# A post-norm decoder layer: smaller selection allowance ahead of normalisations, first carried sum ahead of the rotation, weights in two loads, values last in TensorE's band steps

## The reference

```
proj = x @ w_in + b_in
dq, dk, dv, iq, ik, iw, sq, sk, sv = split(proj)          # rope on dq, dk, iq, ik, sq, sk
score[t, s] = sum_h iw[t, h] * relu(iq[t, h] . ik[s])     # s <= t, 8 index heads
keep the 256 best keys of each query; softmax attention over them, 8 heads share dk, dv
sliding-window attention of 128 keys over sq, sk, sv, 8 heads, 2 key heads, sinks
x = LN(a*x + concat(both) @ w_o)
x = LN(a*x + cross_attention(x, mem))                     # 4 heads of 256, 256 memory tokens
x = LN(a*x + square(relu(x @ w_up)) @ w_down)
```

## Time and profile before

| | us |
|---|---|
| median of 3 runs | 1494.96 |
| lowest and highest | 1489.4, 1495.07 |
| the profiled execution, its own time | 1495.45 |
| its span, first to last instruction | 1493.6 |
| mean granted TensorE clock | 0.993 |

### The profile page before, as it was taken

The page is one execution under the profiler, slowest core; times in us unless marked ns, Lnnn a source line. Parts: engine busy times, 40 slices in busy tenths (PEclk is TensorE's granted clock), DMA queues, the critical chain, the costliest instruction groups (busy, mean ns, idle before and its releaser), DMA issues.

```text
span 1493.6 us, 21073 instructions
## 1 busy us (share of the span) xinstructions
PE 1451.2 (97%) x7552; PEld 1238.0 (83%) x7552; DVE 1070.8 (72%) x2091; ACT 499.6 (33%) x1050; POOL 750.3 (50%) x583
## 2 busy tenths in 40 slices
PE   7999998999899999999999999999999999999997
PEld 7878788999899987888878788888888888888885
DVE  6678899888886334944339677776777777777757
ACT  3135688988776521212202212111111111111111
POOL 4340368677500033044430676766677767867612
PEclk9999999999899999999999999999999999999999
DMA  6446266666310053021111012020201111020202
GB/s 245 165 146 169 85 210 197 177 193 204 108 43 1 1 191 99 22 85 57 57 48 37 7 51 85 3 84 29 85 29 57 57 57 57 29 85 1 85 29 85
DMA packets 61478, 128.98 MB, mean 86 GB/s; under 512 B 6976, under 2 KB 34112, under 8 KB 53696
## 3 DMA queue, kind: packets, MB, share of 16 engines
q1 hardware_dynamic: 51008, 108.76, 22.2%
q10 hardware_dynamic: 10368, 18.88, 3.5%
HBM read 100.35 MB, written 27.26 MB: 85 GB/s over the span
## 4 chain that ended last, share of the span: by engine, by line
PE 91%; DVE 5%; POOL 2%; issue 1%; ACT 1%; DMA 0%; DVEq 0%; ACTq 0%; SPq 0%; POOLq 0%
PE banks L903 25%; PE banks L905 25%; PE banks L904 25%; PE banks L1112 4%; PE banks L960 3%; PE banks L961 2%; PE banks L1099 2%; PE banks L1121 2%; PE banks L1068 2%; POOL w_lo L814 1%; PE banks L1048 1%; POOL w_hi L809 1%; DVE score L1817 0%; DMA raw<-w_v_dram 0%; DVE h_buf L2197 0%
## 5 line engine op out<-in xcount | busy, mean ns | idle before, releaser
L809 POOL TENSOR_SCALAR w_hi<-raw 128x512 fp32r<-128x512 f32 x156 | 103.7, 693 | 409.5 <-PE banks L905 211.1
L2322 DVE TENSOR_TENSOR h_buf<-h_buf,banks 128x512 f32<-128x512 f32 x320 | 202.5, 678 | 13.2 <-PE banks L905 9.7
L814 POOL TENSOR_TENSOR w_lo<-raw,w_hi 128x512 fp32r<-128x512 f32 x156 | 206.9, 1359 | 0.0
L903 PE MATMUL banks<-act_hi,w_hi 128*128 128x512 f32 x512 | 199.9, 390 | 1.7 <-DVE act_lo L2176 1.7
L904 PE MATMUL banks<-act_lo,w_hi 128*128 128x512 f32 x512 | 199.9, 390 | 0.0
L905 PE MATMUL banks<-act_hi,w_lo 128*128 128x512 f32 x512 | 199.8, 390 | 0.0
L903 PE MATMUL banks<-seven_hi,hid_hi 128*128 128x512 f32 x392 | 152.6, 389 | 0.0
L904 PE MATMUL banks<-seven_lo,hid_hi 128*128 128x512 f32 x392 | 152.5, 389 | 0.0
L905 PE MATMUL banks<-seven_hi,hid_lo 128*128 128x512 f32 x392 | 152.5, 389 | 0.0
L903 PE MATMUL banks<-w_hi,act_hi 128*128 128x512 f32 x384 | 152.1, 396 | 0.0
L905 PE MATMUL banks<-w_hi,act_lo 128*128 128x512 f32 x384 | 149.8, 390 | 0.0
(11 more groups left out here) (222 smaller groups left out, 3489.0 us busy)
## 6 DMA issues: line engine op xcount, KB each, us to landing
raw<-w_down_dram SPq DMA_DIRECT2D x16, 1024.0 KB, 4.7
raw_up<-w_up_dram SPq DMA_DIRECT2D x14, 1024.0 KB, 4.8
q_tile<-qk_dram SPq DMA_DIRECT2D x176, 64.0 KB, 2.7
qk_dram<-q_hi ACTq DMA_DIRECT2D x28, 256.0 KB, 2.1
qk_dram<-roped ACTq DMA_DIRECT2D x28, 256.0 KB, 2.6
x_raw<-x_t_dram SPq DMA_DIRECT2D x8, 512.0 KB, 8.9
raw<-wk_mem_dram SPq DMA_DIRECT2D x4, 1024.0 KB, 5.1
raw<-wv_mem_dram SPq DMA_DIRECT2D x4, 1024.0 KB, 5.8
```

The costliest lines, as they stand in the source:

```text
L809: pool.tensor_scalar(w_hi[s][:, col], source[:, col], 1.0, 1.0, ALU.mult, ALU.mult)\
L814: pool.tensor_tensor(w_lo[s][:, col], source[:, col], w_hi[s][:, col].bitcast(F32), ALU.subtract).then_inc(w_ready, 1)
L903: pe.matmul(dst, lh, rh, start=(first and n == 0), stop=False)
L2322: ins = dve.tensor_tensor(out, out, ring_m[g % 6][:], ALU.add if way > 0 else ALU.subtract)
```

## The change

The budget of the band steps gets four values by n % 4 instead of one. SP loads the first weights in two pieces, the first quarter (400 of 1600 columns) first, with a semaphore of its own, for which ACT waits ahead of the first piece; it waits for the rest ahead of the second. In the odd halves DVE does the first carried sum ahead of rope_second. PE's band step does the transposes ahead of the first memory product, and any third product ahead of the values.

```diff
-NARROW_EARLY, BUDGET_BAND = 0.9, 2.1
+NARROW_EARLY = 0.9
+BUDGET_BAND = [2.5, 2.5, 2.5, 0.9]
...
-            sp.dma_start(raw[0][:, 0:columns_of(0)], source_of(0)).then_inc(raw_in[0], 16)
+            rest = slice(v_piece(1).start, columns_of(0))
+            sp.dma_start(raw[0][:, v_piece(0)], source_of(0)[:, v_piece(0)]).then_inc(v_first_in, 16)
+            sp.dma_start(raw[0][:, rest], source_of(0)[:, rest]).then_inc(raw_in[0], 16)
...
                 pieces = pieces_at(n)
+                if 0 <= n - 3 < NS:
+                    swa_turn(n - 3)
                 for use, piece in pieces[0:1]:
                     memory_product(use, piece)
-                if 0 <= n - 3 < NS:
-                    swa_turn(n - 3)
                 if 0 <= n - 2 - NS < ND:
                     turn_probs(n - 2 - NS)
                 for use, piece in pieces[1:2]:
+                    memory_product(use, piece)
+                for use, piece in pieces[2:]:
                     memory_product(use, piece)
                 if 0 <= n - 4 < NS:
                     swa_values(n - 4)
                 if 0 <= n - 3 - NS:
                     times_values(n - 3 - NS)
-                for use, piece in pieces[2:]:
-                    memory_product(use, piece)
...
             round_x(0)
+            act.wait_ge(v_first_in, 16)
+            round_v_weights(0)
             act.wait_ge(raw_in[0], 16)
-            round_v_weights(0)
...
                 carried = index_carried(v + 1)
+                for n in carried[0:1]:
+                    index_sum(n)
                 rope_second(r)
                 for part in range(2):
-                    for n in carried[part:part + 1]:
+                    for n in carried[1:2] if part else ():
                         index_sum(n)
                     if r < POOL_SPLIT:
                         split_roped(r, part)
...
-                    select_for(BUDGET_BAND if n < NS else BUDGET_DSA[DSA[min(n - NS, ND - 1)][0]], True)
+                    select_for(BUDGET_BAND[n % PAIRS] if n < NS else BUDGET_DSA[DSA[min(n - NS, ND - 1)][0]], True)
```

More of the change, by code:

```diff
@@ L508, in build_layer @@
         mem_in = sem("mem_in")
+        v_first_in = sem("v_first_in")
         x_in = sems("x_in", NK)
```

## The result

The changed kernel takes **1509.31 us** (median of six runs, 1502.69 to 1510.53); the kernel before, beside it, 1492.12 us (1488.68 to 1495.07). The ratio is 1.0105, 95% interval 1.0086 to 1.0124: slower by about 1%. The same kernel beside the later experiments took 1506.92 us against 1493.04, ratio 1.0090 (1.0073 to 1.0106). The forecast was 1505, with 1495 to 1511 around it.

A forecast was written before the change was run, and what follows sets the result against it. PE was taken to bound the kernel, busy 1451.2 of 1493.6 us. Terms -0.2 + 7.0 + 3.4 - 1.0 - 0.3 + 1.4 = +10.3 on the median of 1494.96 gave 1505 us, range 1495 to 1511.

The forecast's parts named there:

- The forecast's case: Whole kernel: new PE waits in the index stage, low clock behind, a late split in step 35; 1505 us, chance 0.57.
- Early sum: Index stage, halves 10 to 16: rotation waits for the first rectified score, delaying PE; +6.75, with DVE's queueing +7.0 us.
- small queueing of DVE: Index stage: small extra on DVE that takes the sum of the halves from +6.75 to +7.0 us.
- Half 16: Index stage: score already rectified, so PE's 2.71 us wait moves one score on; gain 0.2 us, bounds 0 and 1.
- Its clock: PE's clock in the index stage: two of three new waits followed by 1.7 us lost; +3.4 us, bounds 0 and 5.1.
- Transposes first: Band steps: a transpose fills time in which PE waits for weights; -1.0 us, bounds 0 and 3.4 gained.
- loads: Kernel start: a smaller first weight piece lets DVE's split, and so PE, begin earlier; -0.2 us, bounds 0 and 0.2.
- Allowance: Band steps: step 7's normalisation wait goes, -0.3; step 35's split comes late, step 36's wait shrinks, net +1.4 us.
- three-product part: Band steps: moving a third product ahead of the values does nothing, as no band step has three products.
- waits without the clock: Rival: index stage +7.0, no added low clock, step 35's split not late; 1497 us, chance 0.2.
- the edits trade evenly: Rival: PE's later waits for POOL and normalisation take up the index delay; 1498 us, chance 0.1.
- faster: Rival: halves 10 to 16 have scores rectified before DVE reaches the rotation, so the early sum frees PE; 1485 us, chance 0.13.

The follow-up runs named there:

- the wait alone: Kernel before, sums left in place; DVE only waits ahead of the rotation until ACT has rectified the first carried score: 1504.84 us, ratio 1.0081.
- half 10 alone: Kernel before with the first carried sum ahead of the rotation only in half 10: 1498.48 us, ratio 1.0027.
- the candidate: Kernel before with first weights in two loads, transposes first, old sum order, and separate allowances for band steps 35 to 39: 1490.10 us, ratio 0.9974.

## Why the prediction was right, and where its terms were off

The forecast's case came in: three new waits at L960 of 3.5, 3.3 and 2.3 us, low stretches behind, a wait of 3.0 us in step 35, and 1505 given for 1509 and 1507. By its steps:

- **Early sum, +7.0.** PE's waits for sums (L1813 and L1817 of the kernel before) were 3.1 + 1.4 = 4.5 us; after, 12.5 + 0.6 = 13.1: +8.6. That the standing is the cause is shown by two runs, the wait alone and the early sum alone. By halves: at 10 the wait grew by 3.2 (given 2.8), at 12 by 2.5 (1.65), at 14 by 2.3 (2.5). Behind the early sum, 16 cost 0.2 more (-0.2) and 17 has a wait of 0.46 that was given nothing; a wait of 0.40 to 0.46 us stands there in the five profiles that have no low stretch behind half 16, and in none of the nine that have one: PE at full clock comes by sooner. The small queueing of DVE (0.25) is in these.
- **What made halves 10 and 12 longer.** From the start of the rotation in the kernel before (here of the first sum) to the end of the second sum, with the first sum in between in both, it took 5.7 and 5.8 us, and now 6.7 and 6.5. It is not that POOL is met for the first time: DVE's first split (L1774, now L1779) met POOL's w_lo operations before as well. What changed is how much of POOL's operation was left when DVE came. Here half 12, DVE and POOL before, then now:

```profile
106.96 1.10 DVE L1774 TENSOR_TENSOR roped<-roped,q_hi 128x512 fp32r<-128x512 f32 x1
105.81 1.71 POOL L814 TENSOR_TENSOR w_lo<-raw,w_hi 128x512 fp32r<-128x512 f32 x1
...
113.28 1.75 DVE L1779 TENSOR_TENSOR roped<-roped,q_hi 128x512 fp32r<-128x512 f32 x1
112.76 1.71 POOL L818 TENSOR_TENSOR w_lo<-raw,w_hi 128x512 fp32r<-128x512 f32 x1
```

POOL's operation ended at 107.52 and at 114.47, and DVE's 0.55 us behind it both times (108.07 and 115.02, by the unrounded records). At half 10 the split took 1.75 instead of 1.25, and the rotation's L1768 1.48 instead of 1.08, ending 0.55 us behind POOL's again. The Trainium skill (SBUF — State Buffer, SBUF: two separate sides) calls this an exclusive lock: a DVE operation with two SBUF inputs and a POOL operation that reads SBUF shut each other out, and the one that starts first keeps the other waiting for its whole length. The trace agrees: of the rotation's and the splits' operations in the kernel before, 16 began well inside a POOL operation, and all 16 ended 0.54 to 0.55 us behind its end, where alone they take 0.69. The prediction used the rule for half 14 only; halves 10 and 12 needed it too, with the time at which DVE would now come.
- **Half 16, -0.2.** The route was right: the wait of 2.71 became 2.57, one score on, and a small one of 0.36 followed. The edit there alone brought nothing.
- **Its clock, +3.4.** The bound of 5.1 was three times 1.7, but a low stretch can be twice as long. The trace of the kernel before had one already, which the prediction did not read, behind the wait of 2.37 us until 395.86:

```profile
396.40:403.20 6.80, 6.80 (x33) 6.61 (x31) 4.45 (x10) 2.82 (x9) 2.95 (x3) 0.50 0.22 61
```

In the early sum alone three stretches of 3.4 us came in the index stage and that behind half 16 went: 9.7 us of busy time at half speed less 3.4, halved, +3.2. In the changed kernel's first profile, with two of the long ones, it was +5.4. Over the whole run and all executions the early sum alone has only about +2.0 (table above). So the term came near in one stage of one profile and was too large for the run of that edit alone.
- **Transposes first, -1.0, and loads, -0.2.** Neither can be told from nothing in the time. The waits for POOL fell by 2.2 us, more than was taken, and the total did not. For the loads, PE's first matmul was given 7.97 and came at 7.82 and 7.14; with one load it came at 7.74 in the middle of nine profiles, so 8.17 was a late start to reckon from.
- **Allowance, -0.3 + 1.4.** Right: +1.6 measured alone (0.3 to 3.1) for the +1.1 given, and by the route given. The three-product part was empty, as said.

All edits but the early sum were given -0.1 in sum (-0.2 - 1.0 - 0.3 + 1.4) and gave +0.6, which is not told from zero. Against the kernel before beside it the whole came to +17.2 and +13.9 us for the +10.3 given (the absolute time agrees better, as the kernel before came out 2 to 3 us under the median the forecast started from). That is luck: 1511 stood 16 us over that median, and +17.2 lies outside of it, +13.9 inside. Of the first miss 1.6 is the waits for sums, 2.0 in the first profile the clock, and 0.7 the other edits, though that is within the noise; the remaining 2.6 us are not in the pair of profiles, whose spans differ by 14.1, and are scatter of the executions around them. Of the rivals, *waits without the clock* had step 35 not late, against the 3.04 us shown, though for the early sum alone its view of the clock was the nearer one; *the edits trade evenly* fell with half 10 alone, of whose 4.4 us nothing was made good; the *faster* one needed DVE late at every half, and DVE stood idle 6.72, 3.37 and 3.84 us before its first sums at 10, 12 and 14.

## What to carry to other kernels

Before moving an operation forward on an in-order engine, compare when its input is done with when the engine comes by, at every place that the edit touches: if the input is later, everything ready behind it pays the difference (here as much for the bare wait as for the moved sum). Where another engine's operations hold up this one's, work out how much of them is left at the new time, not only whether they meet. Where a planner spreads small work by allowances, look at the single steps in which a matmul waits: an allowance for each of the last five steps won where a cycle of four did not.

## What the runs showed of the hardware beyond what was expected

- The same kernel, with waits equal to 0.2 us in sum, had 17.0 us of low clock in its index stage in one execution and 10.2 in another; their spans were 1507.7 and 1503.4. One profile is no measure of the clock's share; the clocks of all executions are a better one.
- Waits of TensorE of like length were followed by a low clock in one profile and not in another: behind the 2.71 us of half 16 lie 3.4 us at 0.51 in the kernel before and none with two loads alone (1.00 from 150 to 160 us); behind 1.95 us in step 36, 3.4 us at 0.50 in the kernel before and none there (1.00 from 376 to 386). A wait of 1.67 us until 833.04 had 3.4 us at 0.50 behind it.
- Keeping TensorE at work in three waits kept its clock at 1.00 there, and did not shorten the run.
- A DVE TENSOR_TENSOR with both inputs in SBUF that began inside a POOL operation ended with POOL's, even when it was small: 128x512 0.54 to 0.55 us behind its end, 128x1 0.01 to 0.02 us behind it. The latter took 0.44 to 1.28 us (L1922 after, beside w_hi; L1915 in the earlier trace rows, beside w_lo). The scaling of 512 columns, with one such input, took 1.47 with POOL at work and 0.48 in the candidate, where it began 0.05 us after POOL's last operation had ended.
